# Seven block products in place of eight in the feed-forward linears of a fused transformer kernel

## What is computed

```python
def swiglu(x, w_gate, w_up, w_down):
    return (jax.nn.silu(x @ w_gate) * (x @ w_up)) @ w_down
...
    x = layer_norm(ALPHA * x + mix.astype(x.dtype), ln_mix_g[i], ln_mix_b[i])
    x = layer_norm(ALPHA * x + swiglu(x, w_ffn_gate[i], w_ffn_up[i], w_ffn_down[i]), ln_ffn_g[i], ln_ffn_b[i])
```

## Time and profile before

| | before |
|---|---|
| median of 3 runs | 2412.04 us (2410.62 to 2412.43) |
| span of the profiled execution (no other time of it was taken) | 2416.8 us |
| TensorE busy with matmuls | 2295.2 us (95%) |
| VectorE, ScalarE, GpSimd busy | 682.9, 399.3, 73.2 us |
| matmul passes of L391 on `x_res` and on `first_arena` | 2560 and 1088 |
| moved by DMA | 619.04 MB |

### The profile page before, as it was taken

The page is one execution under the profiler, slowest core; times in us unless marked ns, Lnnn a source line. Parts: engine busy times, 40 slices in busy tenths (PEclk is TensorE's granted clock), DMA queues, the critical chain, the costliest instruction groups (busy, mean ns, idle before and its releaser), DMA issues. The chain is left out here.

```text
span 2416.8 us, 31143 instructions
## 1 busy us (share of the span) xinstructions
PE 2295.2 (95%) x13007; PEld 1523.4 (63%) x13007; DVE 682.9 (28%) x1476; ACT 399.3 (17%) x832; POOL 73.2 (3%) x81
## 2 busy tenths in 40 slices
PE   8999999999899999998999999999999999989998
PEld 7888788877688877887743333333333333358886
DVE  4242200135400032626422222222232222252222
ACT  2210110014100003224211111111111111123331
POOL 0110100000000000012000000000000000000000
PEclk9999999999999999999999999999999999999999
DMA  6334644455754454310679999999999999953422
GB/s 267 124 122 139 234 151 148 151 213 184 293 196 147 144 196 150 122 54 2 269 309 428 428 428 428 428 428 428 428 428 429 427 428 428 427 215 106 160 70 87
DMA packets 60987, 619.04 MB, mean 256 GB/s; under 512 B 6784, under 2 KB 8064, under 8 KB 12288
## 3 DMA queue, kind: packets, MB, share of 16 engines
q1 hardware_dynamic: 59184, 611.08, 63.3%
q10 hardware_dynamic: 1712, 6.63, 0.8%
HBM read 616.63 MB, written 1.05 MB: 256 GB/s over the span
## 5 line engine op out<-in xcount | busy, mean ns | idle before, releaser
L391 PE MATMUL ps<-x_res,ring 128*128 128x256 f32 x2560 | 567.5, 383 | 21.3 <-ACT x_res L962 12.9
L391 PEld LDWEIGHTS ps<-x_res,ring 128*128 128x128 f32 x2560 | 489.1, 192 | 92.6 <-issue 17.4
L2841 PE MATMUL ps<-expert_ring,moe_xg 128*64 128x512 f32 x1024 | 229.0, 594 | 24.8 <-DMA expert_ring<-we_dram 24.8
L391 PE MATMUL ps<-first_arena,ring 128*128 128x256 f32 x1088 | 239.2, 382 | 3.0 <-DMA ring<-w_o_dram 3.0
L2841 PE MATMUL ps<-ring,moe_xg 128*64 128x512 f32 x1024 | 227.9, 594 | 5.1 <-DMA ring<-we_dram 5.1
L391 PEld LDWEIGHTS ps<-first_arena,ring 128*128 128x128 f32 x1088 | 208.5, 192 | 32.2 <-DMA ring<-w_o_dram 3.5
L2871 PE MATMUL ps<-expert_ring,mix_y 128*64 128x512 f32 x1024 | 226.8, 595 | 0.0
L391 PE MATMUL ps<-third_h,ring 128*128 128x256 f32 x768 | 176.7, 387 | 5.6 <-ACT third_h L274 4.3
L2841 PEld LDWEIGHTS ps<-expert_ring,moe_xg 128*64 128x64 f32 x1024 | 71.6, 137 | 171.1 <-issue 124.5
L2841 PEld LDWEIGHTS ps<-ring,moe_xg 128*64 128x64 f32 x1024 | 72.1, 137 | 150.8 <-issue 125.3
L391 PEld LDWEIGHTS ps<-third_h,ring 128*128 128x128 f32 x768 | 147.8, 194 | 28.6 <-issue 6.8
(11 more groups left out here) (554 smaller groups left out, 1933.0 us busy)
## 6 DMA issues: line engine op xcount, KB each, us to landing
expert_ring<-we_dram SPq DMA_DIRECT2D x128, 2048.0 KB, 22.0
ring<-we_dram SPq DMA_DIRECT2D x64, 2048.0 KB, 24.4
ring<-w_in_dram SPq DMA_DIRECT2D x55, 1024.0 KB, 4.9
ring<-ffn_up_dram SPq DMA_DIRECT2D x44, 1024.0 KB, 4.8
ring<-ada_dram SPq DMA_DIRECT2D x36, 1024.0 KB, 5.0
ring<-w_out_dram SPq DMA_DIRECT2D x16, 1024.0 KB, 5.0
ring<-ffn_dn_dram SPq DMA_DIRECT2D x16, 1024.0 KB, 4.9
ring<-ple_g_dram SPq DMA_DIRECT2D x8, 1024.0 KB, 6.1
```

The source lines that it names most:

```text
L391: mm = pe.matmul(core.ps[:, t % BANKS, 0:TOK], w[:, k * PANEL + c * P:k * PANEL + c * P + P], sources[panel](k0 + k), start=(k0 + k == 0), ...
L2841: mm = pe.matmul(ps[out, bank, :], xg[:, j % 4, j // 4, :], w[:, bank * D + at:bank * D + at + 512], start=False, stop=(j == 7))
```

## The change

In the feed-forward linears a panel is no longer a sum of plain products. It is cut in four quarters: upper and lower half of its row blocks, first and second tile of the pair. The moving side is cut in four too: upper and lower half of the row blocks, first and second 128 tokens. Winograd's arrangement of Strassen's form gets the 2x2 result from seven products of 128x128 blocks, each added up over `kn`/2 row blocks (`SevenProducts.ORDER`), where the plain form has eight. The first pair of each gate-and-up linear stays plain, so there are 21 + 21 panels of `kn` = 8, and all 24 panels of the two down projections.

- GpSimd makes the four sums of the weights of each panel (`sums`), two panels ahead at most (`BUFFERS`), one of them in place in the ring.
- VectorE makes the four sums of the activations (`turn`), once per layer for `x` and once for each of three groups of `h`.
- The seven products lie in two PSUM banks, two sets of banks in turn. ScalarE copies the first product out, VectorE joins the rest in four steps (`combine_first`, `combine_rest`) into `stage`. Silu and the multiplication read `stage` instead of PSUM.
- A down projection no longer adds up over its three panels in PSUM: VectorE adds each panel's result to the residual (`keep`), and the last one by tiles.
- On TensorE the woven programs advance by two tiles after a pair's last panel, since both tiles of a pair end with it.
- The GpSimd part of `BiasParts` goes to VectorE. Eleven semaphores of the expert routing are shared ones, and the scratch of dynamic DMA is 1024.

The diff, cut to its core:

```diff
+    fast = [seven is not None and seven.takes(n, j) for n, j in pairs]
+    fast_panels = [i for i in own if fast[pair_of[i]]]
+    units = [(q, i) for q in range(len(pairs)) for i in own if pair_of[i] == q and (fast[q] or i == last_panel[q])]
+    unit_of = {i: n for n, (_, i) in enumerate(units)}
+    bank_of, reused, user = {}, {}, {}
+    for n, (q, i) in enumerate(units):
+        for c in range(2):
+            bank = seven.SETS[n % 2][c] if seven is not None and pairs[q][0] in seven.names else (2 * q + c) % banks
+            bank_of[n, c], reused[n, c] = bank, user.get(bank)
+            user[bank] = (n, c)
...
+    def wait_bank(pe, n, c):
+        if reused[n, c] is not None:
+            n, c = reused[n, c]
+            q, i = units[n]
+            if fast[q]:
+                pe.wait_ge(seven.combined.sem, seven.combined.at(fast_panels.index(i) + 1))
+            else:
+                wait_tile(pe, 2 * q + c)
...
+                if fast[q]:
+                    wait_bank(pe, n, 0)
+                    wait_bank(pe, n, 1)
+                    half, f = kn // 2, fast_panels.index(i)
+                    for product in seven.ORDER:
+                        bank, at = bank_of[n, seven.PLACE[product][0]], seven.PLACE[product][1] * P
+                        seven.wait(pe, product, f, panel, j, k0)
+                        for p in range(half):
+                            if hook is not None and product in (1, 2):
+                                hook(pe, k0 + p + (product - 1) * half)
+                            mm = pe.matmul(core.ps[:, bank, at:at + P], seven.weight(w, f, half, product, p),
+                                           seven.moving(panel, sources[panel], k0, half, product, p), start=(p == 0), stop=(p == half - 1))
+                        if product == 6:
+                            mm.then_inc(core.first_done.sem, 1)
+                    mm.then_inc(core.panel_used.sem, 1)
+                    if last:
+                        woven.advance()
...
+                if fast[q] and c == 0:
+                    for panel in [panel for panel in own if pair_of[panel] == q]:
+                        f, u = fast_panels.index(panel), unit_of[panel]
+                        if which == "act":
+                            eng.wait_ge(core.first_done.sem, core.first_done.at(u + 1))
+                            seven.copy_first(eng, f, core.ps[:, bank_of[u, 0], 0:P])
+                            continue
+                        if f >= 2:
+                            older = fast_panels[f - 2]
+                            for t in (2 * pair_of[older], 2 * pair_of[older] + 1):
+                                if older == last_panel[pair_of[older]] and order[t][0] == "act":
+                                    wait_tile(eng, t)
+                        seven.combine_first(eng, link, f, core.ps[:, bank_of[u, 0], :])
+                        eng.wait_ge(core.panel_used.sem, core.panel_used.at(panel + 1))
+                        seven.combine_rest(eng, f, core.ps[:, bank_of[u, 1], :])
+                        if panel != last_panel[q]:
+                            seven.keep(eng, link, f, core.stream[panel])
...
+                    if fast[q]:
+                        f = fast_panels.index(last_panel[q])
+                        eng.wait_ge(seven.combined.sem, seven.combined.at(f + 1))
+                        part = seven.tile(f, c)
...
+            if seven is not None:
+                for q in range(len(pairs)):
+                    for f, i in enumerate(fast_panels):
+                        if pair_of[i] == q:
+                            seven.sums(pool, f, i, fast_panels)
+                    woven.advance()
...
+class SevenProducts:
+    ORDER = (1, 5, 7, 6, 2, 3, 4)
+    PLACE = {1: (0, 0), 6: (0, 1), 5: (0, 2), 7: (0, 3), 2: (1, 0), 3: (1, 1), 4: (1, 2)}
+    SETS = ((0, 1), (2, 6))
+    BUFFERS = 2
+    SUMMED = {5: 1, 7: 2, 6: 3, 3: 4}
+    TURNED = {5: 1, 7: 2, 6: 3, 4: 4}
...
+        self.weights = sb("weights", [P, self.BUFFERS, 3, KG // 2, P])
+        self.stage, self.part = sb("stage", [P, 2, 2 * TOK]), sb("part", [P, 3 * P])
+        self.second = sb("second", [P, P])
...
+    def wait(self, pe, product, f, name, j, k0):
+        if product in self.SUMMED:
+            pe.wait_ge(self.summed.sem, self.summed.at(4 * f + self.SUMMED[product]))
+        if product in self.TURNED and j == self.first_pair[name]:
+            pe.wait_ge(self.turned.sem, self.turned.at(4 * self.groups[name, k0] + self.TURNED[product]))
...
+    def sums(self, pool, f, i, fast_panels):
+        core, summed = self.core, self.summed
+        slot, kn = i % RING, core.stream[i][3]
+        pool.wait_ge(core.panel_loaded[slot].sem, core.panel_loaded[slot].at(16 * (i // RING + 1)))
+        if f >= self.BUFFERS:
+            pool.wait_ge(core.panel_used.sem, core.panel_used.at(fast_panels[f - self.BUFFERS] + 1))
+        w = core.ring[:, slot, 0:kn * PANEL].rearrange("p (h k c n) -> p h k c n", h=2, c=2, n=P)
+        a11, a12, a21, a22 = w[:, 0, :, 0, :], w[:, 1, :, 0, :], w[:, 0, :, 1, :], w[:, 1, :, 1, :]
+        s1, s2, s4 = (self.weights[:, f % self.BUFFERS, n, 0:kn // 2, :] for n in range(3))
+        pool.tensor_tensor(s1, a21, a22, ALU.add).then_inc(summed.sem, 1)
+        pool.tensor_tensor(a21, a11, a21, ALU.subtract).then_inc(summed.sem, 1)
+        pool.wait_ge(summed.sem, summed.at(4 * f + 1))
+        pool.tensor_tensor(s2, s1, a11, ALU.subtract).then_inc(summed.sem, 1)
+        pool.wait_ge(summed.sem, summed.at(4 * f + 3))
+        pool.tensor_tensor(s4, a12, s2, ALU.subtract).then_inc(summed.sem, 1)
...
+    def turn(self, dve, n, upper, lower, t1, t2, t3, t4):
+        turned = self.turned
+        b11, b12, b21, b22 = upper[:, :, 0:P], upper[:, :, P:TOK], lower[:, :, 0:P], lower[:, :, P:TOK]
+        dve.tensor_tensor(t1, b12, b11, ALU.subtract).then_inc(turned.sem, 1)
+        dve.tensor_tensor(t3, b22, b12, ALU.subtract).then_inc(turned.sem, 1)
+        dve.wait_ge(turned.sem, turned.at(4 * n + 1))
+        dve.tensor_tensor(t2, b22, t1, ALU.subtract).then_inc(turned.sem, 1)
+        dve.wait_ge(turned.sem, turned.at(4 * n + 3))
+        dve.tensor_tensor(t4, b21, t2, ALU.subtract).then_inc(turned.sem, 1)
...
+    def copy_first(self, act, n, one):
+        if n >= 1:
+            act.wait_ge(self.combined.sem, self.combined.at(n))
+        act.activation(self.part[:, 0:P], one, ACT.Copy).then_inc(self.copied.sem, 1)
+    def combine_first(self, dve, link, n, one):
+        part = self.part
+        dve.wait_ge(self.copied.sem, self.copied.at(n + 1))
+        link(dve.tensor_tensor(self.second[:, :], part[:, 0:P], one[:, P:2 * P], ALU.add))
+        link(dve.tensor_tensor(halves_of(part[:, P:3 * P]), bcast(self.second[:, :].unsqueeze(1), [P, 2, P]), halves_of(one[:, 2 * P:4 * P]),
+                               ALU.add))
+        dve.tensor_tensor(self.stage[:, n % 2, 3 * P:], part[:, 2 * P:3 * P], one[:, 2 * P:3 * P], ALU.add)
+    def combine_rest(self, dve, n, two):
+        dve.tensor_tensor(self.stage[:, n % 2, 0:3 * P], self.part[:, :], two[:, 0:3 * P], ALU.add).then_inc(self.combined.sem, 1)
...
+            if m < 6 and self.alpha != 1.0 and not self.split:
...
+    def keep(self, dve, j, k0, part):
+        x = self.core.x[:, 2 * j:2 * j + 2, :]
+        if k0 == 0 and j < 3:
+            return dve.scalar_tensor_tensor(out=x, in0=x, scalar=self.alpha, in1=part, op0=ALU.mult, op1=ALU.add)
+        return dve.tensor_tensor(x, x, part, ALU.add)
...
+        def turn_x(layer, first, norm):
+            def program(dve):
+                yield first - 1
+                norm.wait(dve, "ready", DT)
+                seven.turn(dve, 4 * layer, core.x[:, 0:4, :], core.x[:, 4:8, :], *(x_turned[:, i, :, :] for i in (0, 2, 1, 3)))
+            return program
...
+        def turn_h(layer, first):
+            def program(dve):
+                for n, k0 in enumerate(range(0, FF_T, KG)):
+                    half = min(KG, FF_T - k0) // 2
+                    yield first + 2 * (k0 + 2 * half) - 1
+                    core.wait_tile(dve, first + 2 * (k0 + 2 * half) - 1)
+                    upper, lower = run.ffn_h[:, k0:k0 + half, :], run.ffn_h[:, k0 + half:k0 + 2 * half, :]
+                    t1, t2, t4 = (h_turned[:, i, k0 // 2:k0 // 2 + half, :] for i in range(3))
+                    seven.turn(dve, 4 * layer + 1 + n, upper, lower, t1, t2, upper[:, :, P:TOK], t4)
```

More of the change, by code:

```diff
@@ L323, in on, with linear @@
         return Woven([program(eng) for program in self.programs[which]])
-def linear(core, name, src, tiles, head=None, act_work=None, pool_work=None, source=None, sync_work=None, weave=None, banks=4):
+def linear(core, name, src, tiles, head=None, act_work=None, pool_work=None, source=None, sync_work=None, weave=None, banks=4, seven=None):
     nc = core.nc
@@ L381, in _ @@
                 hook = hooks.get(panel) if j == 0 else None
-                for c in range(2):
```

(19 more changed lines are left out.)

104 lines of the change are left out of this document (82 added, 22 removed).

## The result

The changed kernel takes **2396.12 us** (median, 2394.3 to 2398.46) against 2412.23 (2410.62 to 2415.23) for the kernel before in the same series: ratio **0.9926 [0.9915, 0.9938]**. The prediction said 2389, in a range from 2368 to 2411. The profiled executions have spans of 2395.9 and 2416.8 us, 20.9 apart. The quotient of the two medians is 0.9933, inside the interval.

The account below looks back on a forecast made before the run. TensorE's pace was taken to bound the kernel: -41.8 us from the passes, plus 2 x (3.2 + 3.1) + 4.5 + 2, makes -22.7; 2412.0 - 22.7 = 2389 us. Range 2378 to 2405 (chance 0.60), 2368 to 2411 (0.80).

Parts of the forecast that it names:

- The pace: Feed-forward linears: 3584 passes of 128 columns at 111.7 ns each replace 2048 of 256 columns, a gain of 41.8 us.
- Rival 2: Fast panels: bubbles, steps of more than 150 ns at each product's first pass; above 2410 us, chance 0.17.
- Rival 4: TensorE passes: a weight load is never hidden, 235 ns a pass, +400 us, 2789 us; chance 0.01.
- Rival 3: Fast panels: GpSimd becomes the bound, a panel's sums taking above 6.26 us; between 2400 and 2425 us, chance 0.12.
- Rival 1: Waits of (a) to (d) mostly hidden, total 2379 us; chance 0.10, given to 2368 to 2378.
- (a): End of each down projection's third pair: TensorE waits for VectorE, 3.2 us per layer (1.5 bare, 1.7 exclusion by GpSimd).
- (b): End of each down projection's fourth pair: TensorE waits for VectorE's addition of tile 6, 3.1 us per layer.
- (c): Before each gate-and-up linear: GpSimd's sums delay VectorE's scalings, 3 us in layer 0, 1.5 in layer 1, 4.5 in all.
- (d): TensorE's granted clock falling behind the new waits: one fall about 1.7 us, up to four added, 2 us taken.

Follow-up runs that it names:

- run 10: The changed kernel with a fifth, unused sum of 512 elements on GpSimd for each panel: 2419.13 us, ratio 1.0022.
- run 7: The changed kernel with GpSimd's first sums held until the norm's scalings are done and each down projection's fourth pair plain: 2377.65 us, ratio 0.984.
- run 1: The changed kernel with GpSimd's sums for each gate-and-up linear's first fast panel held until VectorE's eight scalings are done: 2388.97 us, ratio 0.9901.
- Run 5: The changed kernel with 12, 7 and 8 unused matmuls before TensorE's three waits at the norms behind the down projections: 2392.17 us, ratio 0.9912.

## Why the prediction was right, and where it was off

The forecast was right for its main reason. **The pace** of 111.7 ns, taken from trains of 16 and 28 passes, held over 1638. **Rival 2** (a bubble at each product that begins with a wait) is refuted by the even 0.893 us. **Rival 4** too: here all loads use the same rows, and each is hidden at 111.7 ns a pass. The Trainium skill, TensorE: Matmul & The Clock Gate, "The mechanism", lets a load overlap only where the row group differs; the trace does not agree. (The same section also lets a load go ahead that targets "the background weight buffer", which the prediction left out; no run shows where a load goes.) **Rival 3** did not come about; run 10 shows that it would have with a fifth more of GpSimd's work. The sum was forecast at 1.1 to 1.3 us; it means 1.40 with the time shut out. **Rival 1** did not hold: the waits were there in full.

**(a)** was right in place, size (3.2 forecast, 2.9 and 3.2 measured) and parts: bare 1.5 against 1.57 (run 7), exclusion 1.7 against 1.1. **(b)** was right: 3.1 and 3.1.

**(c)** failed in layer 0. The step was "in layer 0 up to six sums fall between the scalings, 0 to 6.6 us; I take half, 3". The measured 7.35 is above even its upper bound. VectorE and GpSimd take strict turns: one scaling for each sum, every 1.41 us, in each of the seven gaps. Nothing justified the half: GpSimd's sums were ready and waiting. With one sum of 1.1 to 1.3 us in each of the seven gaps, in place of 0.41, the rows gave 4.8 to 6.2; the sums' real 1.41 us makes it 7.0. Here the Trainium skill's page SBUF — State Buffer, "Who interferes with whom", named the mechanism; the trace agrees, with 10.61 us for what took 3.26. In layer 1 the forecast of 1.5 was a gain of 1.0, by the clock: from the first scaling to the side computation's matmuls behind the plain pair it took 9.93 us before, 8.95 after and 8.25 in run 1, so the exclusion itself cost 0.7.

**(d)** was the wrong size: "I take 2 us", measured 8.0. It priced one fall by two windows of the earlier trace rows; there were five, and each cost 1.3 to 2.3 us. Run 5 shows the cause for four of them, the waits.

(c) and (d) together were 8 us too small. In the traces 2.4 elsewhere, the routing part's 3.3 and 0.3 in (a) hide most of that, by luck; on the medians the gain is 16.1 against 22.7, and the kernel 7 us slower than forecast.

Two sums of the rivals were wrong. Rival 1 comes to 2379, inside the band of the forecast and not in the 2368 to 2378 that its chance was given to. Rival 4's 2789 still holds the gain of 41.8 us that its own +400 takes the place of: it should read 2831.

## What to carry to other kernels

Where two engines exclude each other and both have work queued, price it as one whole instruction of the other for each of one's own, and hold the one that has slack behind the other: one wait won 6 to 7 us here. Price a new wait with the clock behind it: the four waits cost 12.3 us, the clock behind them 5.7. Count a faster form's gain per piece against the wait at its end: on the last pairs it gave 1.8 us and cost 4.6, so it belongs where nothing waits for its result.

## What was not expected of the hardware

- Strict turns: eight scalings of 128x256 with two SBUF inputs came every 1.41 us beside GpSimd's sums of 1.3 to 1.45 us (3.26/8 = 0.41 apart without them), and one GpSimd sum took 4.40 us at 334.82, during VectorE's bias subtraction of 32x3072 (4.16 us).
- A GpSimd sum of 128x512 took 1.27 us undisturbed on operands with strides, 1.09 on plain ones.
- The granted clock fell behind waits of 2.7 us, and of 1.6 and 2.0 us close together, but not behind one of 1.57 alone. Behind the 3.2 us of idling ahead of the first gate-and-up linear, with the scalings at 3.26 us, it fell in four profiles and stayed in three. In the routing part identical instructions ran at 0.50 or at 1.00 from one profile to the next.
